# Two of 64 gate items computed after the stage boundary instead of before it, in a fused attention and mixture-of-experts layer

## What is computed

```
proj = h @ w_in[layer]
qa, ka, va, qb, kb, vb, gates = jnp.split(proj, IN_SPLITS, axis=-1)
...
gate = jax.nn.sigmoid((gates + b_gate[layer]).reshape(B, S, N_BRANCH, D))
merged = gate[:, :, 0] * (ya @ w_proj_a[layer]) + gate[:, :, 1] * (yb @ w_proj_b[layer])
x = x + (merged @ w_out[layer]).astype(x.dtype)
h2 = rms_norm(x, norm_ffn_g[layer])
x = x + hierarchical_moe(...)
```

## Time and profile before

| | |
|---|---|
| median of 3 runs | 2416.17 us (2413.89 to 2416.62) |
| the profiled execution's own time | 2416.54 us |
| its span | 2414.7 us |
| mean granted clock of TensorE | 0.989 |
| TensorE busy | 2346.6 us (97%) |
| VectorE, ScalarE, GpSimd busy | 65%, 59%, 28% |

### The profile page before, as it was taken

The page is one execution under the profiler, slowest core; times in us unless marked ns, Lnnn a source line. Parts: engine busy times, 40 slices in busy tenths (PEclk is TensorE's granted clock), DMA queues, the critical chain, the costliest instruction groups (busy, mean ns, idle before and its releaser), DMA issues. The chain is left out here.

```text
span 2414.7 us, 40354 instructions
## 1 busy us (share of the span) xinstructions
PE 2346.6 (97%) x13708; PEld 1935.0 (80%) x13708; DVE 1575.0 (65%) x2303; ACT 1423.3 (59%) x2546; POOL 668.9 (28%) x713
## 2 busy tenths in 40 slices
PE   7999999999999999999999999996999999999997
PEld 6878777778888888888888999985777777777775
DVE  6522555547777777777766334447888788787875
ACT  5323777747776777777753212122677777776775
POOL 0000222134444444444410000000243323333332
PEclk9999999999999999999999999997999999999999
DMA  9687555575655555654356433434899999999995
GB/s 307 203 273 290 192 201 201 145 227 192 207 173 192 185 177 175 203 177 157 116 167 226 131 123 124 130 118 176 322 353 370 352 363 356 357 369 345 368 347 170
DMA packets 204214, 559.03 MB, mean 232 GB/s; under 512 B 21080, under 2 KB 73896, under 8 KB 199216
## 3 DMA queue, kind: packets, MB, share of 16 engines
q1 hardware_dynamic: 179504, 471.01, 55.9%
q0 software_dynamic: 24288, 86.19, 11.8%
q10 hardware_dynamic: 288, 0.07, 0.0%
HBM read 432.87 MB, written 124.32 MB: 231 GB/s over the span
## 5 line engine op out<-in xcount | busy, mean ns | idle before, releaser
L1159 POOL TENSOR_TENSOR sb_sig<-sb_sig,sb_R 128x512 f32<-128x512 f32 (+1 forms) x320 | 333.1, 1041 | 402.2 <-DVE sb_R L1112 402.2
L2369 DVE TENSOR_TENSOR w_region<-ex_w,w_region 128x1024 fp32r<-128x1024 f32 x266 | 305.0, 1220 | 0.0
L1112 DVE TENSOR_TENSOR_SCAN sb_R<-sb_z,sb_R,sb_zeros 128x512 f32<-128x512 f32 x192 | 245.8, 1280 | 69.4 <-ACT sb_z L1055 69.2
L2146 ACT CAST w_region<-ex_w 128x1024 fp32r<-128x1024 f32 x264 | 254.1, 1055 | 0.0
L1054 ACT ACTIVATE sb_sig<-sb_z 128x512 f32<-128x512 f32 (+1 forms) x320 | 171.3, 535 | 127.1 <-PE sb_z L1181 123.3
L1067 ACT CAST sb_aT_hi<-sb_pst 128x512 fp32r<-128x512 f32 (+1 forms) x320 | 167.6, 524 | 100.2 <-PE sb_pst L1188 98.2
L54 PE MATMUL ex_ps_h<-w_region,ex_x_hi 128*128 128x512 f32 x544 | 219.2, 403 | 2.4 <-DVE ex_x_lo L2364 2.4
L1120 DVE TENSOR_TENSOR sb_aT_lo<-sb_pst,sb_aT_hi 128x512 fp32r<-128x512 f32 (+1 forms) x320 | 191.6, 599 | 35.9 <-ACT sb_aT_hi L1067 31.9
L56 PE MATMUL ex_ps_h<-w_region,ex_x_lo 128*128 128x512 f32 x544 | 212.8, 391 | 0.0
L55 PE MATMUL ex_ps_h<-w_region,ex_x_hi 128*128 128x512 f32 x544 | 212.7, 391 | 0.0
L54 PE MATMUL ps_pair<-h_hi,ip_w_hi 128*128 128x512 f32 x448 | 181.4, 405 | 3.1 <-ACT ip_out_hi L549 2.8
(11 more groups left out here) (435 smaller groups left out, 5807.8 us busy)
## 6 DMA issues: line engine op xcount, KB each, us to landing
ex_w<-in_w_exp SPq DMA_DIRECT2D x402, 512.0 KB, 9.2
h_lo<-wg_d SPq DMA_DIRECT2D x126, 512.0 KB, 4.4
gates<-sb_go SPq DMA_DIRECT2D x64, 256.0 KB, 3.7
mo_gates<-gates SPq DMA_DIRECT2D x64, 256.0 KB, 4.2
h_hi<-qk_lo SPq DMA_DIRECT2D x24, 512.0 KB, 7.1
nt_raw<-in_x SPq DMA_DIRECT2D x16, 512.0 KB, 6.1
nt_xT<-in_x_tiles SPq DMA_DIRECT2D x16, 512.0 KB, 4.4
vhl<-nt_vo SPq DMA_DIRECT2D x16, 512.0 KB, 5.3
```

The costliest lines, as they stand in the source:

```text
L1112: nc.vector.tensor_tensor_scan(R[:, r, first + 1:first + width + 1], z[:, j % 3, 0:width], zeros[:, 0:width], start, ALU.mult, ALU.max).th ...
L1159: nc.gpsimd.tensor_tensor(sig[:, j % 5, 0:width], sig[:, j % 5, 0:width], R[:, r, first:first + width], ALU.mult).then_inc(a_done, 1)
L2146: nc.scalar.copy(wu_hi[:, j, :], wr[:, j, :]).then_inc(up_rounded, 1)
L2369: nc.vector.tensor_tensor(wu_lo[:, j, :], wr[:, j, :], wu_hi[:, j, :], ALU.subtract).then_inc(up_split, 1)
```

## The change

`LEFT = 2`. Stick-breaking computes items 0 to 61 (`NI`), but still fetches the weights of all 64 (`NALL`). Items 62 and 63 are computed by TensorE as its first work in the merge (`left_item`); ScalarE applies bias and sigmoid (`take_left`, into `mo_g`, the bias in the first columns of `mo_wr`) and SyncE stores them (`store_left`). So that their operands survive the barrier, SBUF is laid out anew: the region of `wo` now lies over `h0`, and that of `wp` over `gate_w` from piece 4 on. ScalarE therefore waits for every store of yb ahead of its first cast, pieces 2 and 3 are rounded ahead of the second left sigmoid, and piece 4 behind it. PSUM tile `mo_ps` takes the place of `ps_pair`. The wait for all gate stores moves to the place ahead of the first load into `mo_g`.

```
-    NI, NGRP, KP = NG * NC_, KD, KD // 2
+    NALL, NI, NGRP, KP = NG * NC_, NG * NC_ - LEFT, KD, KD // 2
...
-                    if j == max(item_end(it), 0) and 3 <= it + 2 < NI:
+                    if j == max(item_end(it), 0) and 3 <= it + 2 < NALL:
                         load_w(it + 2)
...
-    READ = [range(n + 3, n + 4) for n in range(NO - 3)] + [range(0), range(0)]
+    READ = [range(n + 3, n + 4) if n else range(0) for n in range(NO - 3)] + [range(0), range(0)]
...
-        wo_hi, wo_lo = sb("mo_wo_hi", [P, KD, D], F32R), sb("mo_wo_lo", [P, KD, D], F32R)
+        wo_hi, wo_lo = wo64[:, 0, :, :], wo64[:, 1, :, :]
...
+            def store_left(i):
+                it = NG * NC_ - LEFT + i
+                t, n = divmod(it, NG)
+                sp.wait_ge(left_read, i + 1)
+                sp.dma_start(gates[n, :, t * TC:(t + 1) * TC], left_out[:, it % 2, :]).then_inc(gates_stored[it % 2], 16)
+
             for b in range(2):
                 sp.wait_ge(yb_stored[b], (HB // 2 * NC_ - 1) * 16)
-                sp.wait_ge(gates_stored[b], (NG * NC_ // 2 - 1) * 16)
+                sp.wait_ge(gates_stored[b], (NG * NC_ - LEFT) // 2 * 16)
             load_y(0, 1)
+            sp.dma_start(g_bias, b_gate).then_inc(bias_in, 16)
...
-            for i in range(NS, NS + 3):
-                load_w(i)
+            load_w(NS)
+            store_left(0)
+            load_w(NS + 1)
+            load_w(NS + 2)
+            store_left(1)
             load_w(NS + 3)
             load_gates(NGS)
             load_w(NS + 4)
             load_gates(NGS + 1)
+            for b in range(2):
+                sp.wait_ge(gates_stored[b], NG * NC_ // 2 * 16)
             load_y(1, 0)
             load_y(1, 1)
...
+            def take_left(i):
+                it = NG * NC_ - LEFT + i
+                n = it % NG
+                if i == 0:
+                    act.wait_ge(bias_in, 16)
+                act.wait_ge(left_done, i + 1)
+                nc.scalar.activation(left_out[:, it % 2, :], ps_g[:, it % 2, :], ACT.Sigmoid,
+                                     bias=g_bias[:, n:n + 1]).then_inc(left_read, 1)
+
+            for b in range(2):
+                act.wait_ge(yb_stored[b], HB // 2 * NC_ * 16)
             act.wait_ge(early_in[0], 16)
...
             round_w(1)
+            take_left(0)
+            round_w(2)
+            round_w(3)
+            take_left(1)
             nc.scalar.preload_act_table(ACT.Sqrt)
-            round_w(2)
...
             split_w(2)
+            split_w(3)
...
+            def left_item(i):
+                it = NG * NC_ - LEFT + i
+                v = it % 2
+                pe.wait_ge(w_back[v], it // 2 * 32)
+                for k in range(KD):
+                    last = passes3(nc, ps_g[:, v, :], gate_w[:, 0, v, k, :], gate_w[:, 1, v, k, :],
+                                   h0_hi[:, k, :], h0_lo[:, k, :], k == 0, k == KD - 1)
+                last.then_inc(left_done, 1)
+
+            for i in range(LEFT):
+                left_item(i)
             for u in range(AHEAD):
                 unit(u)
+            pe.wait_ge(left_read, LEFT)
...
+        wo64 = sb("wo_region", [P, 2, KD, D], F32R)
         w64 = sb("w_region", [P, 2, KD, D], F32R)
         low = sb("w_low", [P, 2, KF, D], F32R)
+        logits, cst, b_bc = sb("logits", [P, NT, GR + NE], F32), sb("rt_cst", [P, CW], F32), sb("rt_bias", [P, GR + NE], F32)
```

More of the change, by code:

```diff
@@ L46 @@
 NCOL = MAXB + NE // 4
+LEFT = 2
 NEARLY = 6
@@ L874, in stick_breaking_and_gates @@
 def stick_breaking_and_gates(nc, qk_hi, qk_lo, vhl, h0_hi, h0_lo, head, gate_w, ps_g, hT_d, w, w_first, w_in, wg_d, b_gate, ident_d, neg_ident, mask_d,
-                             ybT, gates, wp_tiles, yaT, first_in_next, old_sems, qk_stored, ya_stored, stored, g_stored):
+                             ybT, gates, wp_tiles, yaT, first_in_next, old_sems, qk_stored, ya_stored, stored, g_stored, w_back):
     QUADS = [(h, g, ch) for h in range(HB) for g in range(NC_) for ch in range(g, NC_)]
@@ L948, in stick_breaking_and_gates @@
         const_in, prep, zeros_set = sem("sb_const_in"), sem("sb_prep"), sem("sb_zeros_set")
-        bias_in, unused = sem("sb_bias_in"), [sem(f"sb_unused{v}") for v in range(4)]
+        bias_in = sem("sb_bias_in")
         head_in, v_in = [sem("sb_head_in0"), sem("sb_head_in1")], [sem("sb_v_in0"), sem("sb_v_in1")]
@@ L954, in stick_breaking_and_gates @@
         quad_done, y2_done, y_read = sem("sb_quad_done"), sem("sb_y2_done"), sem("sb_y_read")
-        w_back = [sem("sb_w_back0"), sem("sb_w_back1")]
+        to_clear = sem("sb_unused")
         h_in = [sem(f"sb_h_in{v}") for v in range(HSLOTS)]
@@ L1241, in _ @@
                     product((j - PROD) // 4)
-    return used[used.index(w_back[0]):]
+    return used[used.index(to_clear):]
 def merge_and_output_projection(nc, yaT, ybT, gates, wp_tiles, wo_d, x, g2, wr_d, ident_d, h2_d, out, logits, cst_d, cst, b_all, b_bc,
                                 stage, early_in, g2T_d, h2_stored, yb_stored, gates_stored,
-                                w64, low, w_pieces, up_rounded, up_split, old_sems):
+                                w64, low, wo64, w_pieces, up_rounded, up_split, old_sems, ps_g, h0_hi, h0_lo, gate_w, w_back, b_gate):
     CT = 2 * P
@@ L1289, in merge_and_output_projection @@
         wr, small = sb("mo_wr", [P, KD, NR]), sb("mo_small", [P, KD + 5])
+        g_bias = wr[:, 0, 0:NG]
+        left_out = g_bc[:, :].rearrange("p (v t) -> p v t", v=2)
         g2T, rstd = small[:, 0:KD], small[:, KD:KD + 2]
@@ L1293, in merge_and_output_projection @@
         x1T = rows[H2T].rearrange("p (k r) -> p k r", k=KD)
+        ps = c.enter_context(nc.psum_tensor("mo_ps", [P, D], F32))
         ps_m = c.enter_context(nc.psum_tensor("mo_ps_m", [P, 3, 2, CT], F32))
-        ps = c.enter_context(nc.psum_tensor("mo_ps", [P, D], F32))
         ps_t = c.enter_context(nc.psum_tensor("mo_ps_t", [P, KD, P], F32))
@@ L1315, in merge_and_output_projection @@
         chosen, marked, ranked = sem("mo_chosen"), sem("mo_marked"), sem("mo_ranked")
+        bias_in, left_done, left_read = sem("mo_bias_in"), sem("mo_left_done"), sem("mo_left_read")
         ps_r = ps_m[:, 0, :, :].rearrange("p b s -> p (b s)")[:, 0:NTA * NE].rearrange("p (t e) -> p t e", t=NTA)
@@ L1860, in routing_and_experts @@
 def routing_and_experts(nc, logits, cst, h2_d, h2_stored, h2_last, w_pieces, ident_d, out, stage,
-                        w64, low, up_rounded, up_split):
+                        w64, low, wr, up_rounded, up_split):
     with ExitStack() as c:
@@ L1867, in routing_and_experts @@
         NA, GA, NL = 2 * NT, 8, NT - NTA
-        wr = sb("ex_w", [P, KD + 2 * KF, D])
         wu_hi, wu_lo = w64[:, 0, :, :], w64[:, 1, :, :]
@@ L2606, in build @@
         h2_stored = c.enter_context(nc.semaphore("mo_h2_stored"))
+        w_back = pair("sb_w_back")
         with ExitStack() as c0:
@@ L2624, in build @@
             sb_sems = stick_breaking_and_gates(nc, qk_hi, qk_lo, vhl, h0_hi, h0_lo, head, gate_w, ps_pair, hT_d, stage, stage_r, sb_w_in, wg_d, b_gate,
-                                     ident, neg_ident, mask, ybT, gates, wp, yaT, mo_w_in, ip_sems, qk_stored, ya_stored, yb_stored, gates_stored)
+                                     ident, neg_ident, mask, ybT, gates, wp, yaT, mo_w_in, ip_sems, qk_stored, ya_stored, yb_stored, gates_stored, w_back)
         sb = lambda n, s, d: c.enter_context(nc.sbuf_tensor(n, s, d))
-        logits, cst, b_bc = sb("logits", [P, NT, GR + NE], F32), sb("rt_cst", [P, CW], F32), sb("rt_bias", [P, GR + NE], F32)
+        with nc.sbuf_tensor("ex_w", [P, KD + 2 * KF, D], F32) as ex_w:
+            pass
+        wo64 = sb("wo_region", [P, 2, KD, D], F32R)
         w64 = sb("w_region", [P, 2, KD, D], F32R)
         low = sb("w_low", [P, 2, KF, D], F32R)
+        logits, cst, b_bc = sb("logits", [P, NT, GR + NE], F32), sb("rt_cst", [P, CW], F32), sb("rt_bias", [P, GR + NE], F32)
         up_rounded, up_split = (c.enter_context(nc.semaphore("ex_" + n)) for n in ("up_rounded", "up_split"))
@@ L2632, in build @@
                                     stage, mo_w_in, g2T, h2_stored, yb_stored, gates_stored,
-                                    w64, low, w_exp, up_rounded, up_split, sb_sems)
-        routing_and_experts(nc, logits, cst, h2, h2_stored, mo_w_in[1], w_exp, ident, out, stage, w64, low, up_rounded, up_split)
+                                    w64, low, wo64, w_exp, up_rounded, up_split, sb_sems, ps_pair, h0_hi, h0_lo, gate_w, w_back, b_gate)
+        routing_and_experts(nc, logits, cst, h2, h2_stored, mo_w_in[1], w_exp, ident, out, stage, w64, low, ex_w, up_rounded, up_split)
 def constants():
```

3 lines of the change are left out of this document (removed).

## The result

| | before | after |
|---|---|---|
| median | 2415.84 us (20 runs, 2413.18 to 2419.47) | 2420.65 us (20 runs, 2418.45 to 2424.27) |
| ratio, 95% interval | | 1.0023 (1.0017 to 1.0029) |
| span of the profiled execution | 2414.7 us | 2422.3 us |

What follows compares the result with a forecast made beforehand. TensorE, busy 2346.6 of 2414.7 us, was taken as the bound, so its idle and slow time mattered. −10.88 + 10.88 − 1.93 − 4.70 − 2.33 = −8.96 us gave a forecast of 2407.5 us, range 2404.5 to 2412.0.

Steps and rivals of the forecast that it cites:

- Stick-breaking gives up all of 10.88: Stick-breaking: TensorE is full there, so removing two gate items takes off all of 10.88 us.
- The rival of the holes: Stick-breaking: removed fill leaves holes, nothing of the 10.88 comes off, 2418.4 us in all; chance 0.02.
- The left items cost 10.88: Head of the merge, before unit 0: the two moved items add 10.88 us at full clock.
- 2.55 us idle: Border of stick-breaking and merge: TensorE idles 2.55 us instead of 4.48, a gain of 1.93.
- Full clock behind it: Merge after the border's idle time: the clock stays full, which gives back 4.70 us.
- ScalarE's later start, its queue and SyncE's are hidden: Start of the merge: delays up to 3 us each in preparing unit 0, and later queue work, stay covered.
- The swap costs nothing more: Swap of the y tiles, unit 7 to 8: the 2.33 us lost there falls to 0.
- the first rival: Swap of the y tiles: unit 5's gates stay late, the 2.33 us stay, 2409.8 us in all; chance 0.22.
- SBUF order, PSUM order [...]: no instruction of the later stages moves; zero.: Later stages: the new SBUF and PSUM order, bias in `wr` and sigmoid output in `mo_g` cost zero.

Runs made afterwards that it cites:

- e2: The changed kernel with rt_cst and rt_bias allocated ahead of the wo, w and low regions and ex_w, putting the regions at multiples of 256: 2408.98 us, ratio 0.9972.
- e6: e2 with the two y loads of chunk 1 issued apart and earlier: 2409.35 us, ratio 0.9974 to the kernel before.
- e7: The kernel of e2 measured once more, unchanged, on the same chip as e6: 2409.89 us, ratio 0.9977 to the kernel before.
- e1: The changed kernel's SBUF layout without the move (LEFT = 0, ScalarE's wait for the last y stores kept): 2428.17 us, ratio 1.0052 to the kernel before.
- e3: The kernel before with rt_cst and rt_bias allocated behind w_region and w_low, putting those two 128 bytes off while wo and ex_w stay: 2426.32 us, ratio 1.0046.

## Why the prediction was wrong

By its own steps, against the changed kernel's trace:

- **Stick-breaking gives up all of 10.88**: right, 10.97 (11.1 from its first score on), with the same 0.6 us of waits for `sb_sig`. The rival of the holes is refuted.
- **The left items cost 10.88**: right, 10.96.
- **2.55 us idle**: right, 2.50.
- **Full clock behind it**: right here and in e2, e6 and e7 (idle 2.50 or 2.51 in each, unit 0 at its full rate), four profiled executions in all. Units 0 and 1 gave back 4.71 of the 4.70.
- **ScalarE's later start, its queue and SyncE's are hidden**: right for units 0 to 7, of which none waited, with less to spare than counted. ScalarE's first cast came 2.8 us behind the barrier (1.2 to 3.3 forecast). The last gate store took 5.3 us to land (2.2 to 4.4 forecast), so that SyncE's first load went out 2.5 us behind the barrier. Piece 4 was split 21.4 us behind it, not by 19.5; 1.1 us were left of the 3.
- **The swap costs nothing more**: wrong; the first rival held, and more. The gates of unit 5 were issued at 1257.15 and taken at 1265.49, after 8.3 us, before after 8.1. The load went out behind that of the first wo piece, which waited for VectorE's split of piece 5:

```profile
1255.50 1.22 DVE L1552 TENSOR_TENSOR w_region<-w_stage,w_region 128x1024 fp32r<-128x1024 f32 x1
```

```profile
1256.75 0.36 SPq L1342 DMA_DIRECT2D w_stage<-in_wo  x1
1257.15 0.47 SPq L1359 DMA_DIRECT2D mo_gates<-gates  x1
```

```profile
1265.49 0.69 DVE L1572 TENSOR_TENSOR mo_gates<-mo_ps_m,mo_gates 128x512 f32<-128x512 f32 x1 [2.03 <-DMA mo_gates<-gates]
```

By the prediction's own count the load would go out 22.9 us behind the barrier, leave 5.3 us of room, and with the old 8.1 us make unit 8 0.8 late; it took zero. The load went out at 24.4 (barrier at 1232.79), since the m of the units comes out of the queue that ran late above. That leaves 3.9 us of room, as before: 0.8 + 1.5 + 0.2 gives 2.5, measured 2.41 (before 2.17). In this execution the clock fell behind the wait as well, 1.5 us more; in e7, behind 2.15 us, it did not.
- **"SBUF order, PSUM order [...]: no instruction of the later stages moves; zero."** This is the step that failed and that turned the gain into a loss. The order of SBUF cost 11.2 us between the changed kernel's trace and e2's, and 11.7 by the medians, more than all gains of the border together; the rest of the 12.9 (4.96 + 7.95) stays in e2. The argument asked only whether instructions move, and whether an address can change what a matmul takes was not asked. No row of the kernel before bounds it; the bound was there to be measured, and the prediction set a zero without one.

With this step put right the same move measured 2408.98 and 2409.89 for a forecast of 2407.5, inside its range. The swap accounts for 1.5 and 2.3 us of what is left (unit 8 follows unit 7 after 4.34 and 5.19 us instead of 2.88). That this matches the 1.5 and 2.4 is partly luck: in these two traces TensorE also waits 0.61 and 1.52 us ahead of the wo products for a split of VectorE, 0.32 before, and two executions of the same kernel end stick-breaking 1.2 us apart (1228.24 and 1229.46). A slip of the sum is small beside it: from the median, 2416.17, the −8.96 give 2407.2, not 2407.5.

The layouts and orders side by side, medians in us. They come from different rounds, in which the kernel before measured 2415.65 to 2416.39:

| | regions at multiples of 256 | 128 off |
|---|---|---|
| items in stick-breaking | 2415.84 (before) | 2428.17 (e1), 2426.32 (e3, wo in place) |
| two items moved | 2408.98, 2409.89 (e2, e7) | 2420.65 (after) |

Leaving e3 aside, the move is worth 6.0 to 7.5 us in either column, and the right column costs 10.8 to 12.3 us in either row (from the kernel before to e1 the order of the regions and ScalarE's wait change as well). In e3 the offset of `w_region` and `w_low` alone costs 10.5.

## What to carry to other kernels

A reordering of SBUF is part of a change's price, even where no instruction moves: compare the addresses of streamed operand and weights, modulo 256, before and after, and pad or permute small tiles until they agree. A busy share of 100% at full clock can hide a slower step; divide a stretch by the matmuls in it, or compare the starts of the same two instructions in both traces. And when a change starts the preparation later, follow what is late through each queue to its last user: here units 0 to 7 hid the delay, but the load of unit 5's gates went out 1.5 us later than counted, and unit 8 waited for it.

## What was not expected of the hardware

- The step of back-to-back 128x512 fp32r matmuls depends on the byte addresses of streamed operand and weights. Where all 48 of a stretch have the same two offsets, it is their difference: modulo 256, a difference of 0 gives 10.98 to 11.01 us for the 48, 64 gives 11.08, 128 gives 11.23, the others from 8 to 240 give 11.18 to 11.35, 4 bytes 11.48. In the layer that is 227 ns against 233 for each, and 0.5% of the whole time; there the addresses of neighbouring matmuls count too (e3). Why, the runs don't show; they show that it needs no other engine, and that it is not where in SBUF the tiles lie.
- Idle times of nearly the same length can end differently for the clock: 2.50 us at the border left it at 2.4 GHz in four profiled executions, 2.41 us at the swap of the changed kernel was followed by 1.2 GHz at 1269.4, and 2.15 us in e7 was not. The Trainium skill, TensorE: Matmul & The Clock Gate, Part 1, calls the monitor free-running against the kernel; these rows agree.
